# Head of a decoder step: the first activations loaded, transposed and split by blocks of 512 channels

## The reference, cut to what matters

```python
hp = concatenate([meta_tokens, x_prompt])      # 16 + 256 tokens, D_MODEL = 2048
hs = x_sample                                  # 8 sequences x 8 tokens
h = x + 0.5 * swiglu(rmsnorm(x, norm_ffn1), w1g, w1u, w1d)      # D_FF = 5632
u = rmsnorm(h, norm_mix)
proj = u @ w_in        # B, C, V, Z, Gc, Gp: conv branch, pool branch, gates, then @ w_o
h = h + merged @ w_o
h = h + 0.5 * swiglu(rmsnorm(h, norm_ffn2), w2g, w2u, w2d)
y = rmsnorm(h, norm_final)

def rmsnorm(x, g): return x * rsqrt(mean(x * x) + 1e-6) * g
def swiglu(x, wg, wu, wd): return (silu(x @ wg) * (x @ wu)) @ wd
```

## Time and profile before

| | before |
|---|---|
| median of 3 runs | 2774.86 us (2774.3 to 2775.12) |
| the profiled execution: time | 2774.16 us |
| its span | 2772.3 us |
| PE busy, of the span | 2757.8 us (99%) |
| DVE, ACT, POOL busy | 1537.4, 1052.8, 12.4 us |

### The profile page before, as it was taken

The page is one execution under the profiler, slowest core; times in us unless marked ns, Lnnn a source line. Parts: engine busy times, 40 slices in busy tenths (PEclk is TensorE's granted clock), DMA queues, the critical chain, the costliest instruction groups (busy, mean ns, idle before and its releaser), DMA issues.

```text
span 2772.3 us, 47809 instructions
## 1 busy us (share of the span) xinstructions
PE 2757.8 (99%) x18725; PEld 2754.3 (99%) x18725; DVE 1537.4 (55%) x2166; ACT 1052.8 (38%) x1283; POOL 12.4 (0%) x22
## 2 busy tenths in 40 slices
PE   9999999999999999999999999999999999999998
PEld 8999999999999999999999999999999999999998
DVE  6555455554555585555555555575555555555555
ACT  5333333333333453333333334363333333333334
POOL 0000000000000000000000000000000000000000
PEclk9999999999999999999999999999999999999999
DMA  6444444444444445444444444454444444444443
GB/s 198 152 145 144 139 149 144 144 144 144 144 145 144 143 136 153 152 148 143 158 141 159 152 151 144 151 159 152 152 151 151 151 151 151 151 151 151 151 151 106
DMA packets 347876, 412.27 MB, mean 149 GB/s; under 512 B 13039, under 2 KB 283503, under 8 KB 347446
## 3 DMA queue, kind: packets, MB, share of 16 engines
q1 hardware_dynamic: 347264, 410.24, 46.9%
q0 software_dynamic: 560, 1.32, 0.2%
HBM read 408.42 MB, written 3.32 MB: 149 GB/s over the span
## 4 chain that ended last, share of the span: by engine, by line
PE 98%; ACT 1%; DVE 0%; issue 0%; DMA 0%; SPq 0%; ACTq 0%; DVEq 0%
PE bank L433 33%; PE bank L434 33%; PE bank L435 32%; DMA acc<-in_x_sample 0%; ACT tb L742 0%; PE bank L686 0%; ACT w_hi L702 0%; SPq L338 0%; DVE w_lo L957 0%; DVE tok L1029 0%; DVE xn_lo L1010 0%; ACT h L761 0%; DVE h L1126 0%; PE bank L660 0%; ACT acc L783 0%
## 5 line engine op out<-in xcount | busy, mean ns | idle before, releaser
L957 DVE TENSOR_TENSOR w_lo<-raw,w_hi 128x1024 fp32r<-128x1024 f32 x772 | 944.0, 1226 | 1021.9 <-ACT w_hi L702 1021.1
L702 ACT ACTIVATE w_hi<-raw 128x1024 fp32r<-128x1024 f32 x772 | 815.6, 1059 | 1322.3 <-PE bank L435 1321.3
L433 PE MATMUL bank<-xn_hi,w_hi 128*128 128x320 f32 (+2 forms) x4224 | 1314.3, 311 | 2.7 <-DVE xn_lo L1010 2.7
L435 PE MATMUL bank<-xn_hi,w_lo 128*128 128x320 f32 (+2 forms) x4224 | 1304.4, 309 | 0.0
L434 PE MATMUL bank<-xn_lo,w_hi 128*128 128x320 f32 (+2 forms) x4224 | 1303.4, 309 | 0.0
L433 PEld LDWEIGHTS bank<-xn_hi,w_hi 128*128 128x128 f32 x4224 | 793.0, 188 | 3.2 <-issue 3.1
L435 PEld LDWEIGHTS bank<-xn_hi,w_lo 128*128 128x128 f32 x4224 | 792.2, 188 | 0.0
L434 PEld LDWEIGHTS bank<-xn_lo,w_hi 128*128 128x128 f32 x4224 | 792.2, 188 | 0.0
L435 PE MATMUL bank<-hid_hi,w_lo 128*128 128x320 f32 (+1 forms) x1952 | 606.4, 311 | 0.0
L434 PE MATMUL bank<-hid_lo,w_hi 128*128 128x320 f32 (+1 forms) x1952 | 604.7, 310 | 0.0
L433 PE MATMUL bank<-hid_hi,w_hi 128*128 128x320 f32 (+1 forms) x1952 | 598.9, 307 | 0.4 <-issue 0.4
(11 more groups left out here) (109 smaller groups left out, 493.2 us busy)
## 6 DMA issues: line engine op xcount, KB each, us to landing
raw<-in_w_ffn_gate SPq DMA_DIRECT2D x176, 512.0 KB, 3.5
raw<-in_w_ffn_up SPq DMA_DIRECT2D x176, 512.0 KB, 3.5
raw<-in_w_ffn_down SPq DMA_DIRECT2D x176, 512.0 KB, 3.6
raw<-in_w_in SPq DMA_DIRECT2D x176, 512.0 KB, 3.5
raw<-in_w_conv_out SPq DMA_DIRECT2D x32, 512.0 KB, 3.9
raw<-in_w_o SPq DMA_DIRECT2D x32, 512.0 KB, 3.7
raw<-in_w_pool_group SPq DMA_DIRECT2D x4, 512.0 KB, 4.2
out<-acc SPq DMA_DIRECT2D x8, 256.0 KB, 3.1
```

The lines of the kernel that those rows point to most:

```text
L433: pe.matmul(out, slot_hi(n, col, col + P), hi, start=start, stop=False)
L435: return pe.matmul(out, slot_lo(n, col, col + P), hi, start=False, stop=stop)
L702: act.activation(slot_hi(n), raw[:, n % RAW, :], ACT.Copy).then_inc(hi_done, 1)
L957: dve.tensor_tensor(slot_lo(n), raw[:, n % RAW, :], slot_hi(n).bitcast(F32), ALU.subtract).then_inc(lo_done, 1)
```

## The change

SP now loads by turns one chunk of weights and 512 channels (a block) of all tokens; the rows of the prompt for block 0 and the meta tokens go by ACT's queue. The tokens in `rows` keep the prompt's own tiling: tiles 0 and 1 are prompt tokens, tile 2 holds the samples and the meta tokens. For each channel tile k, PE transposes four pieces (128, 128, 64 and 16 tokens) into one of six banks; ACT and DVE make the halves straight from that bank, and then copy it to `h` (two tiles of four on each engine). Block 0 is transposed ahead of the first projection, blocks 1 to 3 within it, before k = 2, 6 and 10. The gain of the first norm is loaded and transposed by itself; the others are transposed with the spreading of 1/rms. Squares, mean, root and diagonals are moved behind the first projection's work on ACT and DVE; `spread_rstd` goes from k = 8 of the first projection to k = 12 of the second; the first `silu` goes to the end of the second. The second group of nine products is gone from its place, and the first has eighteen. Chunks 0 to 3 are issued in the head, and the first turn is written out on SP, ACT and DVE.

```diff
@@ sync
+            first_weights(0)
+            sp.dma_start(vecs_in[0:16, :], norm_ffn1.rearrange(flat).rearrange("(k p) -> k p", p=P)
+                         ).then_inc(gain_in, 16)
+            x_columns(0)
+            for b in range(1, 4):
+                first_weights(b)
+                x_columns(b)
@@ gpsimd
             pool.wait_ge(tok_sq, 3)
-            pool.wait_ge(x_copied, 12)
+            pool.wait_ge(x_copied, 8)
+            pool.wait_ge(x_copied_act, 8)
@@ tensor
+            def turn_x(b):
+                pe.wait_ge(x_in[b], 48 if b == 0 else 32)
+                for k in range(4 * b, 4 * b + 4):
+                    if k >= T_BANKS:
+                        old = k - T_BANKS
+                        pe.wait_ge(xn_done, old + 1)
+                        if old % 4 < 2:
+                            pe.wait_ge(x_copied, old // 4 * 2 + old % 4 + 1)
+                        else:
+                            pe.wait_ge(x_copied_act, old // 4 * 2 + old % 4 - 1)
+                    for t, a, z, at in x_parts:
+                        last = pe.transpose(x_bank[k][:, at:at + z - a], rows[a:z, t, k * P:k * P + P], ident[a:z, a:z])
+                    last.then_inc(x_turned, 1)
...
             def spread_rstd():
+                pe.wait_ge(vecs_in_done, 16 * 5)
+                pe.transpose(bank[7][:, 0:P], vecs_in[:], ident[:]).then_inc(vecs_turned, 1)
                 pe.wait_ge(ones_done, 1)
                 pe.wait_ge(diag_done, 3)
...
-            pe.wait_ge(x_copied, 8)
-            keep_busy(PRODUCTS_THEN)
+            keep_busy(PRODUCTS_FIRST)
+            pe.wait_ge(gain_in, 16)
+            pe.transpose(bank[0][:, 0:16], vecs_in[0:16, :], ident[0:16, 0:16]).then_inc(gain_turned, 1)
+            turn_x(0)
...
-            ffn(N_FFN1, 0, 0, (SUM_AT - 2, spread_rstd))
+            ffn(N_FFN1, 0, 0, {4 * b - 2: lambda b=b: turn_x(b) for b in (1, 2, 3)}, {12: spread_rstd})
@@ scalar
+            act.dma_start(rows[:, 0:2, 0:512], x_prompt[0].rearrange("(t p) d -> p t d", p=P)[:, :, 0:512]
+                          ).then_inc(x_in[0], 16)
+            act.dma_start(rows[SAMP:SAMP + META, 2, :], meta_tokens).then_inc(x_in[0], 16)
...
+            for b in range(4):
+                split(b)
+                for k in range(4 * b, 4 * b + 4):
+                    act.wait_ge(x_turned, k + 1)
+                    act.activation(x_hi(0, k), x_bank[k][:, 0:T], ACT.Copy,
+                                   scale=vecs[:, G_FFN1 + k:G_FFN1 + k + 1]).then_inc(xt_hi, 1)
+                for k in (4 * b + 2, 4 * b + 3):
+                    act.wait_ge(xn_done, k + 1)
+                    act.activation(h[:, k, :], x_bank[k][:, 0:T], ACT.Copy).then_inc(x_copied_act, 1)
...
+                    first = {
+                        1: square_rows(0),
+                        2: square_rows(1),
+                        3: square_rows(2),
+                        PROJ: lambda n: root(0, tok[:, 1, :], tok[:, 3, :]),
@@ vector
+            dve.wait_ge(gain_turned, 1)
+            dve.tensor_copy(vecs[:, 0:16], bank[0][:, 0:16]).then_inc(gain_done, 1)
+            dve.wait_ge(gain_done, 1)
+            for b in range(4):
+                split(b)
+                for k in range(4 * b, 4 * b + 4):
+                    dve.wait_ge(xt_hi, k + 1)
+                    dve.scalar_tensor_tensor(out=x_lo(0, k), in0=x_bank[k][:, 0:T],
...
+                for k in (4 * b, 4 * b + 1):
+                    dve.tensor_copy(h[:, k, :], x_bank[k][:, 0:T]).then_inc(x_copied, 1)
...
+                    first = {
+                        PROJ: mean_of_rows,
+                        PROJ + 1: diagonals,
+                        2 * PROJ - 1: rstd_and_silu,
```

More of the change, by code:

```diff
@@ L69 @@
 SUM_AT = 10
-PRODUCTS_FIRST, PRODUCTS_THEN = 9, 9
+PRODUCTS_FIRST = 18
 N_FFN1 = 0
@@ L261, in build @@
                 for x in (ta, tb)]
-        X_ROWS = ((0, P), (P, P), (2 * P, T - 2 * P))
+        T_BANKS = 6
+        x_bank = [bank[2 + k % T_BANKS] for k in range(KD)]
+        x_parts = ((0, 0, P, META), (1, 0, P, META + P), (2, 0, SAMP, META + SEQ), (2, SAMP, SAMP + META, 0))
         Y_ROWS = ((META, P), (META + P, P), (META + SEQ, SAMP))
@@ L448, in project @@
                         k = 4 * c + kk
-                        if between is not None and k == between[0]:
-                            between[1]()
+                        if between is not None and k in between:
+                            between[k]()
                         if norm is not None:
@@ new lines, in spread_rstd @@
+            def spread_rstd():
+                pe.wait_ge(vecs_in_done, 16 * 5)
+                pe.transpose(bank[7][:, 0:P], vecs_in[:], ident[:]).then_inc(vecs_turned, 1)
+                pe.wait_ge(ones_done, 1)
+                pe.wait_ge(diag_done, 3)
+                for t, a, z, at in x_parts:
+                    n = P if t < 2 else SAMP + META
+                    last = pe.matmul(bank[6][:, at:at + z - a], ones[0:n, :], tb[0:n, t, a:z], start=True, stop=True)
+                last.then_inc(rstd_in, 1)
@@ L514, in _ @@
+            pe.sem_inc(used, SLOTS)
             pe.wait_ge(ident_done, 1)
             keep_busy(PRODUCTS_FIRST)
[L518 to L542, removed]
-            pe.wait_ge(x_copied, 8)
-            keep_busy(PRODUCTS_THEN)
-            pe.sem_inc(used, SLOTS)
@@ new lines, in mean_of_rows, with diagonals @@
+            def mean_of_rows(n):
+                dve.wait_ge(tok_set, 1)
+                dve.wait_ge(tok_sq, 3)
+                mean(tok[:, 0, :], tok[:, 1, :]).then_inc(root_in, 1)
+            def diagonals(n):
+                stepped(inverse_root(0, tok[:, 1, :], tok[:, 2, :], tok[:, 3, :], tok[:, 4, :]))
+                dve.wait_ge(ident_done, 1)
+                for t in range(3):
+                    count = P if t < 2 else SAMP + META
+                    dve.tensor_scalar(tb[0:count, t, 0:count], ident[0:count, 0:count],
+                                      tok[0:count, 4, t:t + 1], None, ALU.mult).then_inc(diag_done, 1)
@@ L1144, in ffn @@
                     last[4 * PROJ + SPREAD_ENDS[q]] = add_half(q, next_norm)
-                stage(n0, FFN_TURNS, FFN_CHUNKS, (4, 4, 8, 0, 0, 12), lambda i: work, last)
+                stage(n0, FFN_TURNS, FFN_CHUNKS, (4, 4, 8, 0, 0, 12), lambda i: work, last, first)
             ffn(N_FFN1, 0, 1)
```

184 lines of the change are left out of this document (104 added, 80 removed).

## The result

| | before | after |
|---|---|---|
| median | 2774.53 us (9 runs, 2774.04 to 2775.45) | 2782.01 us (9 runs, 2780.80 to 2783.27) |
| profiled execution: time, span | 2774.16, 2772.3 | 2781.49, 2779.6 |

What follows compares the result with a forecast made beforehand. PE was taken to bound the kernel, so only the head counted: +0.8 us with the wait for the diagonals and +2.5 for the clock gave +3.3, 2777.5, predicted as 2778.0. The forecast's own range was 2776.3 to 2779.7.

Steps and rivals of the forecast that it cites:

- transposes of a block: PE's transposes of one block inside the first projection: 0.33 us a tile, 1.3 a block, 3.9 for three.
- mean held until: DVE's mean, due 0.35 us after POOL's clearing of `acc` starts, is held until that ends at 41.68.
- PE's wait: At k = 12 of the second projection PE waits for the diagonals from 40.1 to 45.9, 5.8 us.
- lost to the clock: After PE's wait the clock falls and steps are twice as long: 2.5 us lost, bounds 1.7 to 4.3.
- second projection over, against before: End of the second projection against the kernel before: +0.8 from the wait and +2.5 from the clock, +3.3.
- the mark: Where PE went on after the second projection before, 49.65 us; the forecast put it +3.3 later.
- a sign of being wrong: The forecast is wrong if, among other signs, the part behind 60 us differs by more than 0.5.
- the rival of the late block 0: Block 0 comes only at 10 or later, everything shifts by 1 to 2 us: 2779.5, chance 0.07.
- the clock needs 8.7 us each time: Slow clock: first transposes slow too (+1.2), more lost after the wait (+1.8): +6.3, 2781, chance 0.08.
- The mean gets in ahead: DVE's mean precedes POOL's clearing; PE's wait is 2, too short for a clock fall: -3, 2771.5, chance 0.17.
- nothing waits: PE alone bounds the head, without a wait for the diagonals: -4.9, 2769.6, chance 0.03.
- slower: Outcome above 2780.4 us, beyond 0.2%: the slow clock and the upper end of the late block, chance 0.11.

Runs made afterwards that it cites:

- three pieces: Changed kernel with the token tiles of before (128, 128 and 80 tokens for each channel tile), x loads cut to match: 2776.83 us, +2.1 against the kernel before.
- POOL late: POOL's state loads and memset also wait for the three diagonals: 2776.37 us in the changed kernel, 2773.06 us in the kernel before.
- its eight variants: Changed kernel with edits, alone or combined, to token pieces, POOL's wait, root's place, chunk 0's order or added products: medians from 2770.79 to 2779.84 us.
- x first: The fastest kernel with chunk 0 of the weights issued behind the gain and the x of block 0: 2772.52 us (0.9991).
- the 15 products at the wait: Changed kernel with 15 products of the identity in front of PE's wait for the diagonals: 2779.84 us (1.0020).
- the fastest kernel: Changed kernel with pieces of 128, 128, 80, POOL behind the diagonals, and mean, root, diagonals ahead of the split of chunk 7: 2770.79 us (0.9986).
- both cures: The fastest kernel with the x of block 0 ahead of chunk 0, and 22 products of the identity at the start in place of 18: 2772.97 us (0.9993).
- the first series: Kernel before, its first products replaced by 30 products and eleven series of identity transposes, eight rounds each, two products behind each: 2811.45 us, one run.
- root early: Mean, root and diagonals moved ahead of the split of chunk 7, on the changed kernel with three pieces and POOL late: 2770.79 us (0.9986).
- The second series: Kernel before with identity transposes in place of its first products, four rounds of each pattern, 34 products behind every series: 2867.04 us, one run.

## Why the prediction was wrong

| step | forecast | profiled |
|---|---|---|
| products end | 8.3 | 8.0 |
| x of block 0 there | 6 to 7 | 8.8 |
| first product | 10.6 | 11.8 |
| transposes of a block | 1.3 | 2.9 |
| k = 12 of the second projection | 40.1 | 46.5 |
| sum of the third square | 35.4 | 40.1 |
| mean held until | 41.7 | 46.0 |
| diagonals there | 45.8 | 49.8 |
| PE's wait | 5.8 | 3.2 |
| lost to the clock | 2.5 | 1.6 |
| second projection over, against before | +3.3 | +6.5 |

The step that failed is a term of the sum: "pieces of 64 and 16 are not in the trace. They lie between nothing and 0.083; I take 0.05 each, so 0.33 for a tile". A tile costs 0.73. The upper end was wrong in kind, not only in size. It took the price of a piece to be its own, when the price is that of the neighbours it stands between: even the two pieces of 128 cost more here than in the earlier trace rows: from start to start 0.17 for the one that follows a piece of 16 rows and 0.20 for the one that stands before a piece of 64. PE came to k = 12 6.4 us later than forecast: 1.2 at the first product (block 0's own transposes and its late x), 4.8 in three blocks of 1.6 more, 0.4 in the steps of the products. ACT's squares were held back by less (4.7), so the wait shrank by 2.6, and the clock cost 0.9 less: 6.4 - 2.6 - 0.9 is 2.9 of the 3.2 by which the mark was missed. The kernel with three pieces shows the same from the other side: with that term at its forecast size, the time is +2.1, inside the range. Of the 4.0 us by which the time was missed the other 0.8 lies behind the second projection, more than the 0.5 that I had named as a sign of being wrong; other kernels show as much there without any tie to an edit. The forecast's last step has a slip as well: 2777.5 and 0.7 are 2778.2, not 2778.0.

The mechanism named beside it held. The mean was held by POOL's memset to within 0.03 us of its end, PE waited, the clock fell, and it came back after 3.4 us, the lower bound I had given from the head. I had put the mean's lag behind the memset's start at 0.35; it was 0.64. With POOL late in either kernel it is gone. The traces agree with the rule of the Trainium skill (SBUF — State Buffer, Who interferes with whom) that the engine which starts first blocks the other fully: the memset had started first each time, and the mean took 2.40 and 3.78 us with it running, 0.16 without.

Block 0 came 2 us later than I had worked out. I took 2 us before the first bytes and then a full rate. The windows of the changed kernel have 230 GB/s in 2 to 4 us, 314 in 4 to 6 and only 198 in 6 to 8. It cost about 0.6, beside the larger block of transposes ahead of the first product. It was there before 10, so the rival of the late block 0 didn't happen either.

Of the rivals, "the clock needs 8.7 us each time" is out: the rise in the head came at about 6.5 us (36 matmuls in 6.58 us are 23 at 0.213 and 13 at 0.114), and the second low stretch lasted 3.4. The forecast took that rise from one trace; its place scatters. In the changed kernel and its eight variants PE begins in the same way and has no pause in its products, yet their steps go to 0.114 at 4.5 in one (x first) and only at 7.7 in another (with the 15 products at the wait). So the same eighteen products end between 7.2 and 8.7. Nor was it safe to call a wait of 2 us too short for a fall: the pauses of 1.97 in the fastest kernel and of 1.91 with both cures were followed by one, and those of 1.71 with three pieces and of 2.12 in the first series (58.1 to 60.2) were not. "The mean gets in ahead" and "nothing waits" didn't happen here; the last is what the fastest kernel does, at 2770.8 against the 2769.6 that the forecast gave it.

The sign was as forecast but the size crossed the bound of 0.2%: the chance that I gave to slower, 0.11, was meant for a slow clock, and no case held a wrong price of the transposes.

## What to carry to other kernels

Give an instruction that the trace doesn't show a price only with its neighbours, and let the range take in that it slows them: 128, 128, 64 and 16 rows cost 0.72 us where 128, 128 and 80 cost 0.29. When a step is moved, look at what runs on POOL at the new place: a three-element operation of DVE took as long as what was left of a 4.4 us memset, and one more wait on POOL gave 5.8 us. Splitting loads finer paid only when both were mended, and then, with the root early, 2.3 us beyond what the one wait gives the kernel before (2770.8 against 2773.1, on one chip).

## What the runs showed of the hardware

- PE's clock can fall without a pause of PE. In the first series of transposes it fell at about 21.6, behind pieces of 128 and 64 rows that had followed one another without a gap from 17.83 to 21.46, and was back at 38.7: four products took 0.71 us before, 1.22 among them and 0.71 at the end. The second series, with 7.8 us of products between the patterns, never showed it.
- Where the clock rises or falls varies by microseconds between executions that begin alike: the first rise came between 4.5 and 7.7 us, and of four pauses of PE of 1.7 to 2.1 us ahead of the second projection two were followed by a fall.
- Transposes of 64 or of 16 rows in series of one height are cheap (0.10 and 0.09 us); alternated with 128 rows they cost 0.22 and 0.20 for each piece, the one of 128 included, and with one another 0.18. With 128 and 80 rows by turns a piece costs 0.09.
- A three-element operation of DVE was held until a memset on POOL ended (3.78 us in place of 0.16), and with it the split queued behind it (2.33 in place of 1.22 in the kernel before).
